# A two-layer decoder step: expert weights in idle buffers, a projection computed transposed, and turn 0's down products moved

## The reference

```python
def odd_mixer(h, w_in, ln_w, ln_b, w_s, b_s, w_out):
    z = gelu(h @ w_in)                      # 1024 -> 4096
    u, v = z[..., :2048], z[..., 2048:]
    v = layer_norm(v, ln_w, ln_b)
    w_m = where(idx[:, None] >= idx[None, :], w_s, 0.0)     # 8 groups of 128x128
    mixed = einsum('hts,ncshd->ncthd', w_m, v) + b_s        # over 128 positions
    return (u * mixed) @ w_out, v           # 2048 -> 1024

def hier_moe(h, w_rg, w_re, w_gate, w_up, w_down):
    # 4 groups of 8 experts: best group, in it the two best experts, weights from softmax
    act = silu(h @ w_gate[e]) * (h @ w_up[e]) * gates       # 1024 -> 256, for 32 experts
    return sum over e of act @ w_down[e]                    # 256 -> 1024
```

## Time and profile before

| What | us |
|---|---|
| median of three timed runs (lowest, highest) | 1045.35 (1044.04, 1046.35) |
| the profiled execution, and its span | 1042.79, 1041.1 |
| even mixer | 0 to 366 |
| MoE layer 0 | 366 to 596.1 |
| odd mixer | 596.1 to 803.3 |
| MoE layer 1, last norm, stores | 803.3 to 1041.1 |
| busy in the span: PE, VectorE, ScalarE, GpSimd | 955.7, 424.0, 237.6, 89.1 |

### The profile page before, as it was taken

The page is one execution under the profiler, slowest core; times in us unless marked ns, Lnnn a source line. Parts: engine busy times, 40 slices in busy tenths (PEclk is TensorE's granted clock), DMA queues, the critical chain, the costliest instruction groups (busy, mean ns, idle before and its releaser), DMA issues.

```text
span 1041.1 us, 18468 instructions
## 1 busy us (share of the span) xinstructions
PE 955.7 (92%) x6934; PEld 573.8 (55%) x6934; DVE 424.0 (41%) x1105; ACT 237.6 (23%) x513; POOL 89.1 (9%) x199
## 2 busy tenths in 40 slices
PE   8999989899989999997798799999999999978985
PEld 7777767676885375543463344444544755524532
DVE  3732555554855345452544200252112464424533
ACT  3321135453401042111110311241001411100102
POOL 6333232041000000000000000000000000000000
PEclk9999999999989999998999999999999999988997
DMA  9961177784904699999999975533649399999995
GB/s 288 247 185 44 43 226 243 277 318 188 341 2 157 235 342 384 422 419 418 422 420 415 353 247 162 162 123 121 252 155 403 146 390 420 421 418 420 421 411 184
DMA packets 96846, 292.63 MB, mean 281 GB/s; under 512 B 16739, under 2 KB 57243, under 8 KB 70862
## 3 DMA queue, kind: packets, MB, share of 16 engines
q1 hardware_dynamic: 82292, 267.64, 67.5%
q0 software_dynamic: 5152, 17.05, 5.2%
q10 hardware_dynamic: 9306, 6.67, 2.0%
HBM read 286.17 MB, written 5.16 MB: 280 GB/s over the span
## 4 chain that ended last, share of the span: by engine, by line
PE 75%; DMA 9%; DVE 6%; SPq 5%; ACT 2%; issue 2%; ACTq 0%; DVEq 0%
PE ps L1734 11%; PE ps L985 10%; PE ps L1455 7%; DMA arena<-in_moe_w_up 7%; PE ps L1469 6%; PE ps L1824 5%; SPq L493 3%; PE ps L1099 3%; PE ps L1524 3%; PE ps L1582 2%; PE ps L909 2%; PE ps L1488 2%; PE ps L1112 2%; PE ps L900 2%; PE ps L1188 2%
## 5 line engine op out<-in xcount | busy, mean ns | idle before, releaser
L1469 PE MATMUL ps<-arena,hT 128*32 128x512 f32 x768 | 93.7, 644 | 21.6 <-DMA arena<-in_moe_w_up 21.6
L1734 PE MATMUL ps<-arena,hT 128*128 128x512 f32 x256 | 111.0, 593 | 0.0
L985 PE MATMUL ps<-hT,arena 128*128 128x288 f32 x448 | 110.0, 407 | 0.0
L1455 PE MATMUL ps<-lvl,htok 128*128 128x128 f32 (+1 forms) x768 | 95.4, 281 | 6.6 <-DVE x L2724 6.5
L1455 PEld LDWEIGHTS ps<-lvl,htok 128*128 128x128 f32 x768 | 90.2, 191 | 15.5 <-issue 10.6
L985 PEld LDWEIGHTS ps<-hT,arena 128*128 128x128 f32 x448 | 84.6, 190 | 23.5 <-issue 0.5
L1734 PEld LDWEIGHTS ps<-arena,hT 128*128 128x128 f32 x256 | 48.3, 190 | 59.7 <-issue 59.4
L1469 PEld LDWEIGHTS ps<-arena,hT 128*32 128x32 f32 x768 | 26.7, 118 | 83.1 <-issue 82.7
L1524 PE MATMUL ps<-arena,cst 128*32 128x512 f32 x448 | 51.0, 595 | 1.3 <-ACT cst L2110 1.3
L2710 DVE TENSOR_SCALAR hT<-ps,nw 128x128 f32<-128x128 f32 (+1 forms) x64 | 22.7, 355 | 66.4 <-PE ps L1455 66.1
L1824 PE MATMUL ps<-arena 128*128 128x512 f32 x112 | 49.2, 592 | 0.0
(11 more groups left out here) (516 smaller groups left out, 1332.9 us busy)
## 6 DMA issues: line engine op xcount, KB each, us to landing
arena<-in_moe_w_gate SPq DMA_DIRECT2D x64, 1024.0 KB, 19.7
arena<-in_moe_w_up SPq DMA_DIRECT2D x56, 1024.0 KB, 18.0
arena<-in_moe_w_down SPq DMA_DIRECT2D x48, 1024.0 KB, 21.6
arena<-in_cache_k SPq DMA_DIRECT2D x64, 256.0 KB, 4.0
arena<-in_cache_v POOLq DMA_DIRECT2D x64, 256.0 KB, 4.0
arena<-in_w_in_odd SPq DMA_DIRECT2D x16, 1024.0 KB, 11.1
arena<-in_w_in_even SPq DMA_DIRECT2D x14, 1024.0 KB, 9.0
arena<-in_moe_w_down SPq DMA_DIRECT2D x48, 256.0 KB, 5.4
```

Source lines behind the costliest of these rows:

```text
L985: last = mm(ps[:, c % 4, 0:T], w[:, k, P * (c % 2):P * (c % 2 + 1)], hT[:, k, :], start=k == 0, stop=k == KD - 1)
L1455: last = mm(ps[:, row_bank(k), 0:w], htok[:, i, P * k:P * (k + 1)], pl[:, i, 0:w], start=i == 0, stop=i == 2)
L1469: last = mm(ps[EC * j:EC * (j + 1), q % 2, :], xgT[q % 2][:, k, EC * j:EC * (j + 1)], ring[:, sl:sl + 2, DE * k:DE * (k + 1)], start=k == ...
L1734: last = mm(ps[:, bank, :], hT[:, k, P * i:P * (i + 1)], ring[:, oslot(2 * n):oslot(2 * n) + 2, QC * k:QC * (k + 1)], start=k == 0, stop=k ...
```

## The change

Three things. **First**, units 4 and 5, the ups of turn 0's first two experts, no longer go to the ring: `homes` are nine pieces of other buffers, idle at that time, that hold their 16 pieces of 128 KB between them, and `homes_load` loads them, in nine DMAs, at the end of both fills. Slots 4 and 5 start with units 24 and 25, the first gate and up of turn 2. Their expert, number 8, is so fixed, and `SWAPPABLE` is one higher. The order in `fill_odd` follows the new mixer. **Second**, u is computed transposed: the stationary operand is a block of 128 weight columns, the moving one is `hTn`, all 288 tokens of hT with the row scale multiplied in (VectorE, from a broadcast that PE makes with `diag`); Gelu writes straight into `uT`. The mixing is transposed as well (`mix(c)`, stationary v, moving mixing matrix), stands between the blocks of the projection (`MIX_AT`), and VectorE adds a bias that a DMA has spread over all partitions, and multiplies. `product_rows` is gone. **Third**, `down(0)` stands after the third of the eight gather pieces, and `act_turn(0)` after the second.

```diff
-SWAPPABLE = QE * X_TURN
+SWAPPABLE = QE * X_TURN + 1
...
+        hTn = wk(6144, KD, T)
...
+        homes = [(cst[:, 512:1536], 4), (work[:, M + 384:M + 1408], 4), (lfp[:, :, :, :].rearrange("p a b c -> p (a b c)"), 2),
+                 (cst[:, 0:256], 1), (neg2[:, :], 1), (wsm[:, :, :].rearrange("p k c -> p (k c)"), 1),
+                 (lvl[:, :, :].rearrange("p a b -> p (a b)")[:, 608:864], 1),
+                 (cs27[:, :, :].rearrange("p c w -> p (c w)")[:, 0:256], 1),
+                 (wr[:, 0, :, :].rearrange("p k c -> p (k c)")[:, 0:256], 1)]
...
+        AT_HOME = [QE, QE + 1]
+
+        def up_piece(j, k):
+
+            return HOMES[KD * j + k][2]
...
-        in_slot = [[w for p, w in enumerate(SEQ) if p % RSLOTS == sl] for sl in range(RSLOTS)]
+        in_slot = [[w for p, w in enumerate(SEQ) if p % RSLOTS == sl and p not in (QE, QE + 1)] for sl in range(RSLOTS)]
...
+            if isinstance(r, int) and u in AT_HOME:
+                eng.wait_ge(s.up_home, 16 * len(homes) * (layer + 1))
+            elif isinstance(r, int):
                 wait_first(eng, layer, ("unit", u))
...
+        MIX_AT = {8: (0, 1, 2), 9: (3, 4, 5), 10: (6, 7, 8), 11: (9, 10, 11), 12: (12,), 13: (13, 14), 14: (15,)}
+
+        def mix_no(c):
+
+            return c + (2 if c < 3 else 3)
...
-                    sp.wait_ge(s.gm_u_ps, u_no("s0" if j < 12 else "s1" if j < 14 else (3, 1)))
+                    sp.wait_ge(s.gm_u_ps, 2 * (j - 8) + 2)
...
+            def homes_load(layer):
+                for i, (tile_, n_pieces) in enumerate(homes):
+                    if i == len(homes) - 1:
+                        sp.wait_ge(s.rl_ps, 2 * layer + 1)
+                    at = sum(n for _, n in homes[:i])
+                    for e in range(at // KD, (at + n_pieces - 1) // KD + 1):
+                        k0, k1 = max(at - KD * e, 0), min(at + n_pieces - KD * e, KD)
+                        c0 = KD * e + k0 - at
+                        sp.dma_start(tile_[:, DE * c0:DE * (c0 + k1 - k0)],
+                                     WU[layer, e:e + 1].rearrange("e (p k) f -> p (e k f)", p=P)[:, DE * k0:DE * k1])\
+                            .then_inc(s.up_home, 16)
...
-                        moe_load(0, 0, u)
+                        moe_load(0, 0, in_slot[u][0][1])
...
+                homes_load(0)
...
-                        moe_load(1, 0, u)
+                        moe_load(1, 0, in_slot[u][0][1])
 
                 sp.wait_ge(s.gm_sum, 6)
                 for u in (14, 15):
                     moe_load(1, 0, u)
-                over_weights(0, 1, 2, 3)
-                moe_load(1, 0, 17)
-                over_weights(4)
-                sp.wait_ge(s.gm_m_ps, HC + 1)
-                moe_load(1, 0, 16)
+                over_weights(0)
+                sp.wait_ge(s.gm_m, mix_no(NU - 1) + 1)
+                for u in (11, 12, 13, 16):
+                    moe_load(1, 0, u)
                 sp.wait_ge(s.out_misc, 16 * 13)
                 for u in (8, 9, 10):
                     moe_load(1, 0, u)
-                over_weights(5)
-                sp.wait_ge(s.gm_t_ps, NU)
-                for u in (11, 12, 13):
-                    moe_load(1, 0, u)
-                over_weights(6, 7)
+                over_weights(1, 2, 3)
+                moe_load(1, 0, 17)
+                over_weights(4, 5, 6, 7)
                 sp.wait_ge(s.x_new, 9)
                 for u in range(18, RSLOTS):
                     moe_load(1, 0, u)
+                homes_load(1)
...
-                for u in range(RSLOTS + QE, MOE_UNITS):
-                    if u == MSLOTS * X_TURN:
+                for u in range(RSLOTS + QE + len(AT_HOME), MOE_UNITS):
+                    if u == MSLOTS * X_TURN + len(AT_HOME):
...
-                                sl = moe_slot(r, (gate_no, up_no)[part](r, q, j))
+                                u = (gate_no, up_no)[part](r, q, j)
+                                w = up_piece(j, k) if u in AT_HOME else ring[:, moe_slot(r, u), DE * k:DE * (k + 1)]
                                 last = mm(ps[EC * j:EC * (j + 1), q % 2, DE * part:DE * (part + 1)],
-                                          xgT[q % 2][:, k, EC * j:EC * (j + 1)], ring[:, sl, DE * k:DE * (k + 1)],
+                                          xgT[q % 2][:, k, EC * j:EC * (j + 1)], w,
...
                         else:
-                            gather(1, range(3))
+                            gather(1, range(2))
                             act_turn(0)
+                            gather(1, range(2, 3))
+                            down(0)
                             gather(1, range(3, KD))
...
-                        else:
+                        elif q:
                             down(q)
...
-                project(0, ev, bank).then_inc(s.gm_v_ps, 1)
-
-            pe.wait_ge(s.ws_loaded, 64)
-            for h in range(HC):
...
-                if h >= 2:
-                    pe.wait_ge(s.gm_t, 2 * h - 2)
+                project_v(ev, bank).then_inc(s.gm_v_ps, 1)
+                if ev == V_ORDER[1]:
+                    pe.wait_ge(s.rr_rows, 1)
+                    for i, (r0, m) in enumerate(TOK):
...
+            def mix(c):
+                h = c // 2
+                if c >= 4:
+                    pe.wait_ge(s.gm_m, mix_no(c - 4))
                 for i in range(2):
-                    last = mm(ps[:, 5 + h % 2, QC * i:QC * (i + 1)], wmT[:, h, :], vrow[:, i, QC * h:QC * (h + 1)],
+                    last = mm(ps[:, c % 4, P * i:P * (i + 1)], vrow[:, i, P * c:P * (c + 1)], wmT[:, h, :],
                               start=True, stop=True)
                 last.then_inc(s.gm_m_ps, 1)
 
@@ -1777,66 +1815,55 @@
                                   vrow[0:TS, 2, QC * h:QC * (h + 1)], start=True, stop=True)
...
+            def turn_samples():
+                pe.wait_ge(s.gm_m, 1)
+                for b in range(4):
+                    last = tr(ps[:, 4, P * b:P * (b + 1)], mixS[:, P * b:P * (b + 1)], ident[:, :])
+                last.then_inc(s.gm_m_ps, 1)
+
+            pe.wait_ge(s.rr_rows, KD + 1)
+            for c in range(NU):
+                if c % 2 == 0:
+                    wait_odd(pe, 8 + c // 2)
+                if c >= 2:
+                    pe.wait_ge(s.gm_u, c - 1)
+                o = P * (c % 2)
+                for k in range(KD):
+                    last = mm(ps[:, 5 + c % 2, 0:T], ring[:, oslot(8 + c // 2), QC * k + o:QC * k + o + P], hTn[:, k, :],
+                              start=k == 0, stop=k == KD - 1)
+                last.then_inc(s.gm_u_ps, 1)
+                if c == NU // 2:
+                    pe.wait_ge(s.gm_sum, 6)
+                    pe.wait_ge(s.ws_done, 2 * HC + 1)
+                    pe.wait_ge(s.gm_v, NPROJ)
+                    mix_samples()
+                for m in MIX_AT.get(c, ()):
+                    mix(m)
+                if c == NU // 2:
+                    turn_samples()
 
...
+                    pe.wait_ge(s.gm_m, mix_no(c))
                     for b in range(4):
+                        if c == 0:
+                            pe.wait_ge(s.gm_m, mix_no(NU - 4 + b))
                         mm(ps[:, b, :], uT[:, c, P * (b // 2):P * (b // 2 + 1)],
                            w[:, e, 512 * (b % 2):512 * (b % 2 + 1)], start=c == 0, stop=False)
+                if j == 0:
+                    pe.wait_ge(s.gm_m, mix_no(NU - 1) + 1)
                 for e in range(2):
...
-            for h in range(HC):
-                product_rows(h)
-                if h:
-                    out_rows(h - 1)
-                if h + 2 < HC:
-                    mix(h + 2)
+            for j in range(HC - 1):
+                out_rows(j)
             wait_odd(pe, 23)
...
-            act.dma_start(bs8[0:HC, :], t["gm_spatial_b"][0]).then_inc(s.ws_loaded, 16)
+            act.dma_start(biasT.rearrange("p h t -> p (h t)"),
+                          t["gm_spatial_b"].rearrange("o h t -> o (h t)").partition_broadcast(P)).then_inc(s.ws_loaded, 16)
...
+            for c in range(NU):
+                act.wait_ge(s.gm_u_ps, c + 1)
+                A_(uT[:, c, :], ps[:, 5 + c % 2, 0:T], ACT.Gelu).then_inc(s.gm_u, 1)
+                if c < 3:
+                    m = TOK[c][1]
+                    act.wait_ge(s.gm_sum, c + 1)
+                    if c:
+                        act.wait_ge(s.gm_sq, c)
+                    A_(sqj[0:m, :], vrow[0:m, c, :], ACT.Square, accum_out=lss[0:m, c:c + 1]).then_inc(s.gm_sq, 1)
...
+            dve.wait_ge(s.rr_done, rms_no(2) + 1)
+            for i, (r0, m) in enumerate(TOK):
+                last = V.tensor_scalar(diag[0:m, i, 0:m], ident[0:m, 0:m], rr[0:m, 6 + i:7 + i], None, ALU.mult)
+            last.then_inc(s.rr_rows, 1)
+            dve.wait_ge(s.hT_act, 4 * 2 + 4)
+            dve.wait_ge(s.hT_dve, 4 * 2 + 4)
+            dve.wait_ge(s.ws_ps, 1)
+            for k in range(KD):
```

(19 more changed lines are left out.)

155 lines of the change are left out of this document (48 added, 107 removed).

## The result

| us | before | after | predicted |
|---|---|---|---|
| median of the runs beside each other | 1044.69 (4) | 1034.74 (4) | 1033.7 |
| profiled execution | 1042.79 | 1034.5 | 1031.2 |
| its span | 1041.1 | 1032.9 | |

What follows compares the result with a forecast made beforehand. PE's instruction list bounds the odd mixer, expert-weight transfers the MoE layers. Odd mixer -8.0, layer 1 -4.1, layer 0 +0.5 make -11.6 us: from 1045.35 to 1033.7 us, range 1029.5 to 1040.0.

Steps and rivals of the forecast that it cites:

- Odd mixer: Whole odd mixer, all PE work on the path: 199.2 us against 207.2, so -8.0 us (bounds -9.0 to +1.5).
- First projection with its inserts: Odd mixer, first projection: inserted transposes and small matmuls take 1.9 us; the 3.6 us stretch behind it goes.
- Turned projection: Odd mixer, second projection: 256 instructions of 288 moving columns at 0.2434 us each, 62.3 us.
- The rival of exposed loads: Odd mixer, second projection: 256 weight loads lie bare and add 48.6 us, giving 1082; chance 0.03.
- Mixes, sample mixes and four transposes: Odd mixer, second projection: mixing matmuls 7.5 us, sample mixing about 1.0, transposes 0.6, plus 0.5 for exposed loads.
- Output: Odd mixer, output stage: seven periods of 7.87 us plus 8.0 for the last, 63.1 us against 75.8.
- The cover: Odd mixer: VectorE ends v's normalisation near 690.4, PE needs it at 695.4, leaving 5.0 us.
- MoE layer 1: Layer 1: 2.10 MB prefetched in the router's gap bring load 32's data at 857.2 instead of 861.2, -4.1 us.
- the gap in the transfers: Layer 1, before load 32: transfers end at 856.3, next data at 857.2, a new gap of 0.9 us.
- MoE layer 0: Layer 0: same bytes in another order, small rows cost 0.5 us, PE waits 1.9 us; +0.5 us (0 to 2).
- The prefetch buys nothing: Layer 1: late gate-up or PE as limit leaves only -8.0 + 0.5, 1037.9 us; chance 0.20.
- serial small transfers: Both MoE layers: the nine small DMAs go one at a time, +9.5 us in all, 1054.9; chance 0.05.

Runs made afterwards that it cites:

- The grouping experiments: Kernel after, layer 0's home DMAs issued before the stored-state wait, output samples grouped in pairs (1033.74 us) or two groups (1031.44 us).
- The kernel with two groups of samples: Kernel after, layer 0's home DMAs before the stored-state wait, output samples in two groups (periods 0 to 3, 4 to 6): 1031.44 us, ratio 0.9875.
- the sixteen homes: Kernel after with each layer's homes moved in sixteen DMAs of 128 KB in place of nine: 1033.12 us, ratio 0.9877.

## Why the prediction was right, step by step

The parts add to -7.4, -3.1 and +0.3, so -10.2 us, against -11.6 predicted and -10.8 measured (-8.1 to -13.4). That the forecast of 1033.7 came within 1.0 us of the median 1034.74 is partly luck: the kernel before ran at 1044.69 beside it, 0.7 us below the 1045.35 from which the forecast was reckoned.

**Odd mixer, -8.0 predicted, -7.4 measured in every profile with the turned projection and single samples.**
- First projection with its inserts: 64.6 us measured, 64.2 predicted.
- Turned projection: 144 instructions from 663.04 to 698.16, and seven groups of 16 at 3.88 to 3.89 us, together 62.3 us; 62.3 predicted. With a load for each instruction, PEld is busy 56.65 of 70.96 us and stays hidden. The rival of exposed loads is dead. The Trainium skill's rule that a load overlaps a matmul only in other row groups (TensorE: Matmul & The Clock Gate, Part 3: Packing small matmuls) does not hold for this shape: all 128 rows are in use in both. The same section also has a load overlap when it goes to the background weight buffer, and with that the trace is compatible.
- Mixes, sample mixes and four transposes: 71.0 less 62.3, 8.7 us, against 9.6 with the allowance for exposed loads. The stretch was 0.9 shorter than predicted.
- Output: 734.00 to 798.18, 64.2 against 63.1. The mis-sized term is the period, 8.06 instead of 7.87. I took 7.87 from the distance of two products less what stood between them, six transposes. With those gone the first large matmuls follow the samples directly, and seven times 0.19 is 1.3 us; the last product was 0.1 shorter than I had. The grouping experiments showed that the loss hangs on the change of tile size.
- The sum came nearer than its terms: +0.4, -0.9 and +1.1 partly cancel, which is luck.
- The cover held: VectorE's last normalisation operation ends at 692.96 (690.68 + 2.28), PE's first mixing matmuls, those of the samples, start at 698.16. 5.2 us, 5.0 predicted. The prediction's "3 to 13% busy" for VectorE in that stage is misread: the three long stretches of the earlier trace rows have 1%, 38% and 12%. Nothing hung on it; after it is 11%, 46% and 9%.

```profile
678.91 0.17 DVE L2928 RECIPROCAL sm<-sm 128x3 f32<-128x3 f32 x1 [8.64 <-ACT sm L2229]
...
690.68 2.28 DVE L2932 TENSOR_TENSOR arena<-arena 32x2048 f32<-32x2048 f32 x1
```

**MoE layer 1, -4.1 predicted, about -3.1 measured.** The steps on PE came as predicted. Relative to the stage's shift of 4.9 us, turn 0's downs start 3.7 us earlier, PE drains exactly the 0.55 us that was priced, and the turn-2 downs are issued at 850.62, where the prediction has 855.96 less 4.9, 851.06:

```profile
834.18 3.64 PE L1556 MATMUL ps<-arena,cst 128*32 128x512 f32 x32
837.75 3.62 PE L1486 MATMUL ps<-lvl,htok 128*128 128x128 f32 x30
841.91 1.49 PE L1535 MATMUL ps<-ident,sm 128*128 128x128 f32 x12 [0.55 <-ACT hT L2123]
843.34 7.07 PE L1500 MATMUL ps<-arena,hT 128*32 128x512 f32 x64
```

The mis-sized term is the gap in the transfers behind it: 0.9 us predicted, 1.7 measured. Besides the 1.0 us from 851 to 853 the queue lacks another 0.6 in the five microseconds behind, where I had it full again at once. Against 422 GB/s the same 23 us lack 1.5 to 2.2 us in all eight profiles with homes and moved downs, 0.1 at most in before and in the turned projection alone, and 0.5 with the moved downs alone. What makes the second dip is open: the four loads that follow the gap had been issued by 854.60. From there on nothing is lost. The last 150 us ahead of the mark move the same bytes before and after:

```profile
864.74:1014.74 150.00, 130.57 (x1084) 64.97 (x1082) 58.94 (x139) 16.63 (x42) 0.00 (x0) 0.95 1.01 418
```

```profile
856.83:1006.83 150.00, 131.92 (x1110) 68.45 (x1108) 59.74 (x141) 17.29 (x43) 0.00 (x0) 0.98 1.01 418
```

So of the 5.0 us that 2.10 MB are worth some 3.3 arrive (5.0 less 1.7). The transfer mark says the same: 210.1 in the mean of three profiles without homes, 206.95 in the mean of seven with homes and moved downs (206.6 to 207.5), so -3.1. The run with the downs in the old place has 206.91. The kernel with two groups of samples, not among the seven, has the smallest gap, 1.5 us, and the lowest mark, 206.08. Two of the signs that the prediction named were missed by a little: the transfers of layer 1 end 3.1 us earlier beyond the mixer's shift, not 4, and PE waits 3.2 us or more ahead of layer 0's first ups, not 1 to 3.

**MoE layer 0, +0.5 predicted.** The marks are 209.4 without homes (208.85, 209.19, 210.23) and 209.7 in the mean of six with them behind the loads: +0.3, in a scatter of about 1. PE's wait was mis-sized, 3.2 to 3.65 us for 1.9: the transfers did not run at full rate from the first issue, but at 346 GB/s from 386 to 390 and 365 from 390 to 400. The wait cost nothing that the marks show, because the stretch is bound by transfers: the next waits shrank from 6.56 and 4.77 to 3.96 and 2.53.

**The moved downs** were priced only together with the homes. Apart from them they bring nothing (1.0014). With them the medians differ by 2.5 us, within the intervals, while the marks are equal and the gaps 1.7 and 1.85 us: the step moved a gap of the queue and hardly shortened it.

**The rivals.** "The prefetch buys nothing" is refuted by the homes and moved downs alone, -4.9 us (-3.1 to -6.8), and by the mark of layer 1; serial small transfers by the sixteen homes; exposed loads by the 62.3 us.

## What the runs showed of the hardware

**PE's clock after a wait is worth up to 2 us at the end of a layer.** The last turn waits twice, for its last ups and ahead of its last downs. Then the first 32 matmuls of these downs run at either clock level or between the two. In the first repetition of after they take 5.09 us at a granted clock of 0.50 (1.2 GHz); in the second 3.30 us at 1.00 (2.4 GHz), 0.49 of it another wait. In the first, PE had waited 3.14 and 1.45 us ahead of them; in the second 3.11 and 0.72. The window of each (length, PE's busy time and instructions, its clock, DMA share, GB/s):

```profile
1012.28:1017.37 5.09, 5.09 (x32) 0.50 0.84 286
```

```profile
1010.00:1013.30 3.30, 2.81 (x32) 1.00 0.82 270
```

From the start of the last downs to the end of the span it is 21.6 us in the first and 19.6 in the second. That is half of the 4.3 us between their spans (1033.9 and 1029.6); the rest is in layer 0, ahead of its mark (210.42 and 208.61).

The same is the +1.5 us of layer 0 in the first pair of profiles. Its last downs (columns as in the earlier trace rows; the first line is before, the second after):

```profile
581.73:585.75 4.02, 4.02 (x33) 1.29 (x33) 0.00 (x0) 0.60 (x1) 0.00 (x0) 0.65 0.94 308
```

```profile
582.74:587.84 5.10, 5.10 (x33) 1.77 (x35) 0.00 (x0) 0.60 (x1) 0.00 (x0) 0.50 0.97 326
```

They are 1.1 us longer, and the four matmuls behind them take 0.92 in place of 0.55. The same kernel has either: behind layer 0's mark it is 21.5 us in this profile of after, 20.3 and 20.1 in its two repetitions, and 20.0 before. With the +0.9 of the even mixer it accounts for the profiled pair being only 8.3 us apart: without these two it would be 10.7, and the ratio of all runs gives 10.8. That is why stages and marks were compared instead of ends. What makes the clock fall in one execution and not in another is open.

**A stall in the middle can cost more than its length.** In the kernel before, PE works less than half of 658.4 to 662.0, waiting for VectorE between transposes, and its clock stayed at 1.00. In the profiled run with the moved downs alone the same stall was as long and stood at 1.00 as well, but right behind it the clock fell (PE's busy time and instructions, its clock, DMA share, GB/s):

```profile
660.00:662.42 2.42, 1.02 (x9) 1.00 0.91 311
662.42:664.00 1.58, 1.58 (x6) 0.65 1.05 355
664.00:665.00 1.00, 1.00 (x3) 0.50 1.10 356
665.00:666.00 1.00, 1.00 (x2) 0.50 1.10 350
666.00:667.00 1.00, 1.00 (x3) 0.85 1.07 341
```

The 64 large matmuls behind the stall take 29.43 us in place of 27.73 before, and that is the 1.7 us by which its mixer is longer (the windows lack 0.55, 0.5, 0.5 and 0.15). The third kernel with this stall, the homes and moved downs alone, kept 1.00. The turned projection removed that stall, and no profile with it shows a fall in the mixer.

**A change between 32-column and 128-column tiles costs 0.34 us** there and back. 0.19 of it is on the large side: sixteen large matmuls take 7.06 us behind samples and 6.87 behind other large ones (13.93 for the 32 of a pair, less 7.06). A 128-column load takes 0.19 us in the same rows; that the loss is the first such load, uncovered, fits but was not isolated.

## What to carry to other kernels

A dense list on PE could be predicted to within 2% in each of its three parts here from rows of the very same shape. The boundaries between shapes have to be counted as well: group matmuls of one tile size, since each change and return cost 0.34 us here. In these runs a stretch bound by transfers became shorter by bytes that moved into an empty gap (2.10 MB, 3.1 us). Putting a load earlier where another transfer was already running moved the wait and won about 1 us by the marks. The gap that such a move opens later is to be measured over a wide window: 1.0 us of it stood in the two microseconds where I had looked, and 1.7 in all. And where a stage's difference is a microsecond or two, run the same kernel again before giving it a cause: layer 0's +1.5 us was there without the part that I had blamed, and had the clock as its cause.
